# Gated feed-forward values brought to their partitions by 32x32 block transposes on VectorE and transfers within SBUF instead of TensorE transposes

## The reference, cut to what matters

```
def swiglu(h, w_in, w_out):
    gate, up = jnp.split(h @ w_in, 2, axis=-1)
    return (jax.nn.silu(gate) * up) @ w_out
```

## Time and profile before

| | us |
|---|---|
| Time, median of 3 executions | 1643.75 |
| Lowest and highest | 1642.6, 1644.36 |
| Profiled execution: its time | 1644.13 |
| Profiled execution: its span | 1642.0 |
| PE busy in the span | 1613.3 |
| DVE busy | 1039.4 |
| ACT busy | 817.1 |
| POOL busy | 570.8 |

### The profile page before, as it was taken

The page is one execution under the profiler, slowest core; times in us unless marked ns, Lnnn a source line. Parts: engine busy times, 40 slices in busy tenths (PEclk is TensorE's granted clock), DMA queues, the critical chain, the costliest instruction groups (busy, mean ns, idle before and its releaser), DMA issues.

```text
span 1642.0 us, 20828 instructions
## 1 busy us (share of the span) xinstructions
PE 1613.3 (98%) x7757; PEld 1334.1 (81%) x7757; DVE 1039.4 (63%) x1054; ACT 817.1 (50%) x983; POOL 570.8 (35%) x368
## 2 busy tenths in 40 slices
PE   6999999999999999999999999999999999999998
PEld 5888888978888788887878888888887888878887
DVE  5455568776665765567777765576667567774454
ACT  5455563354444534456655443553446666563433
POOL 0000100068991499920008897069990000000000
PEclk9999999999999999999999999999999999999999
DMA  7565653347776587864436787657784454545562
GB/s 258 182 201 179 230 175 113 123 146 251 245 250 209 175 260 245 259 213 154 145 112 204 259 258 247 202 186 254 238 269 153 154 166 150 172 152 184 185 196 77
DMA packets 208572, 321.48 MB, mean 196 GB/s; under 512 B 10952, under 2 KB 146434, under 8 KB 208514
## 3 DMA queue, kind: packets, MB, share of 16 engines
q1 hardware_dynamic: 196256, 281.05, 51.7%
q0 software_dynamic: 10512, 38.54, 7.5%
q10 hardware_dynamic: 1746, 1.11, 0.2%
HBM read 319.62 MB, written 1.05 MB: 195 GB/s over the span
## 4 chain that ended last, share of the span: by engine, by line
PE 92%; DVE 4%; ACT 2%; issue 1%; DMA 0%; ACTq 0%; SPq 0%; DVEq 0%
PE ps L557 27%; PE ps L559 26%; PE ps L558 26%; PE ps L603 3%; PE ps L848 2%; PE ps L661 2%; PE ps L611 2%; DVE w_lo L1820 1%; PE ps L565 1%; ACT w_hi L1299 1%; PE ps L1115 0%; ACT arena L1567 0%; DVE arena L1854 0%; DMA raw<-ffn_w_in_dram 0%; PE ps L980 0%
## 5 line engine op out<-in xcount | busy, mean ns | idle before, releaser
L1820 DVE TENSOR_TENSOR w_lo<-raw,w_hi 128x2048 fp32r<-128x2048 f32 x266 | 656.9, 2481 | 274.0 <-ACT w_hi L1299 273.8
L1299 ACT CAST w_hi<-raw 128x2048 fp32r<-128x2048 f32 x266 | 505.3, 1912 | 189.6 <-PE ps L559 187.4
L557 PE MATMUL ps<-w_hi,actT_hi 128*128 128x512 f32 x1456 | 578.2, 397 | 5.6 <-DVE hidden L1960 2.7
L559 PE MATMUL ps<-w_hi,actT_lo 128*128 128x512 f32 x1456 | 568.8, 391 | 0.0
L558 PE MATMUL ps<-w_lo,actT_hi 128*128 128x512 f32 x1456 | 567.8, 390 | 0.0
L557 PEld LDWEIGHTS ps<-w_hi,actT_hi 128*128 128x128 f32 x1456 | 274.0, 188 | 63.4 <-issue 5.7
L559 PEld LDWEIGHTS ps<-w_hi,actT_lo 128*128 128x128 f32 x1456 | 273.7, 188 | 58.6
L558 PEld LDWEIGHTS ps<-w_lo,actT_hi 128*128 128x128 f32 x1456 | 274.0, 188 | 54.0
L526 POOL TENSOR_TENSOR arena<-arena,c_silu 128x1024 f32<-128x1024 f32 x72 | 163.9, 2277 | 124.5 <-DVE actT_lo L1848 59.9
L557 PE MATMUL ps<-w_hi,hT_hi 128*128 128x512 f32 x480 | 187.5, 391 | 0.0
L559 PE MATMUL ps<-w_hi,hT_lo 128*128 128x512 f32 x480 | 186.8, 389 | 0.0
(11 more groups left out here) (258 smaller groups left out, 1323.3 us busy)
## 6 DMA issues: line engine op xcount, KB each, us to landing
raw<-ffn_w_in_dram SPq DMA_DIRECT2D x176, 512.0 KB, 4.8
raw<-ffn_w_out_dram SPq DMA_DIRECT2D x88, 512.0 KB, 4.4
arena<-w_ada_dram POOLq DMA_DIRECT2D x72, 512.0 KB, 5.5
raw<-ffn_w_gate_dram SPq DMA_DIRECT2D x44, 512.0 KB, 3.9
raw<-ffn_w_up_dram SPq DMA_DIRECT2D x44, 512.0 KB, 4.9
raw<-ffn_w_down_dram SPq DMA_DIRECT2D x44, 512.0 KB, 4.3
raw<-w_in_dram SPq DMA_DIRECT2D x40, 512.0 KB, 4.7
raw<-hg_w_in_dram SPq DMA_DIRECT2D x32, 512.0 KB, 4.7
```

The source lines that it names most:

```text
L557: nc.tensor.matmul(to, hi, whi, start=start, stop=False, skip_group_check=True)
L559: return nc.tensor.matmul(to, lo, whi, start=False, stop=stop, skip_group_check=True)
L1299: nc.scalar.copy(w_hi[:, s, :], raw[:, s, :]).then_inc(hi_ready[s], 1)
L1820: nc.vector.tensor_tensor(w_lo[:, s, :], raw[:, s, :], w_hi[:, s, :].bitcast(F32), ALU.subtract)\
```

## The change

The four TensorE transposes of each chunk but the last are gone. In their place:

- `product` writes the gated values in another order of the free dimension: it reads both operands with a stride of four elements and writes runs of 32, so that hidden columns with the same remainder modulo 4 stand together.
- `blocks` on DVE, right behind `product`, transposes the whole tile `hidden` in 32x32 blocks into a region of SBUF, `hid_blocks`.
- `to_columns` on ACT, at the end of the chunk, waits for it and issues four transfers of 64 KB each, SBUF to SBUF, each from 32 partitions to all 128, in pieces of 512 bytes, into `hT_raw`.
- `turned_hi` and `turned_lo` read `hT_raw` in SBUF instead of the PSUM bank. `turned_hi` waits for the transfers.

The last chunk of each sublayer still goes through TensorE. Some semaphores are merged or dropped at the start of the program without a new wait.

```diff
+        hid_blocks, hT_raw = (region(9600 + 512 * i, 4, P) for i in range(2))
+
+        def by_block(r):
+            return r.rearrange("p (f i b) -> p b f i", f=2, b=4)
+
+        def hidden_block(t):
+            return hidden.rearrange("p t f -> p (t f)").rearrange("p (b f t i) -> p t b f i", b=4, f=2, t=TILES)[:, t]
+
+        hT_columns = hT_raw.rearrange("p a (n j) -> p n a j", n=4)
...
-            pool.wait_ge(hT_turned, NF + 1)
+            pool.wait_ge(hT_turned, 2)
...
-                def turn_hidden(c):
-                    pe.wait_ge(hidden_ready, 2 * (n + c + 1))
-                    for f in range(2):
-                        for t in range(TILES):
-                            last = nc.tensor.transpose(ps[:, HT_BANK, f * T + t * P:f * T + (t + 1) * P],
-                                                       hidden[:, t, f * P:(f + 1) * P], ident)
-                    last.then_inc(hT_turned, 1)
...
                 def middle(c):
                     up(c, 0)
-                    turn_hidden(c - 1)
                     up(c, 1)
                     down(c - 1, False)
...
+                def to_columns(c):
+                    g = st.ffn * (NF - 1) + c
+                    act.wait_ge(hid_turned, g + 1)
+                    if positive(g):
+                        act.wait_ge(hT_ready, g)
+                    for a in range(4):
+                        nc.scalar.dma_start(hT_raw[:, a, :], hid_blocks[32 * a:32 * a + 32, :, :]).then_inc(hT_loaded, 16)
+
                 def turned_hi(c):
-                    act.wait_ge(hT_turned, st.ffn * (NF + 1) + c + 1)
-                    nc.scalar.copy(hT_hi[:, :, :], ps[:, HT_BANK, :].rearrange("p (f t) -> p f t", f=2)).then_inc(hT_hi_ready, 1)
+                    act.wait_ge(hT_loaded, 64 * (st.ffn * (NF - 1) + c + 1))
+                    if positive(filled[2] + c):
+                        act.wait_ge(split_used[2], filled[2] + c)
+                    nc.scalar.copy(hT_hi.rearrange("p f t -> p (f t)").rearrange("p (n a j) -> p n a j", n=4, a=4), hT_columns)\
+                        .then_inc(hT_hi_ready, 1)
...
                     split_hi(1, filled[1] + c + 1)
+                    to_columns(c)
...
+                def blocks(c):
+                    g = st.ffn * (NF - 1) + c
+                    dve.wait_ge(hidden_ready, 2 * (n + c) + 2)
+                    if positive(g):
+                        dve.wait_ge(hT_loaded, 64 * g)
+                    nc.vector.transpose(hid_blocks.rearrange("p b n -> p (b n)"), hidden.rearrange("p t f -> p (t f)"))\
+                        .then_inc(hid_turned, 1)
+
                 def turned_lo(c):
                     dve.wait_ge(hT_hi_ready, st.ffn * (NF - 1) + c + 1)
-                    nc.vector.tensor_tensor(hT_lo[:, :, :], ps[:, HT_BANK, :].rearrange("p (f t) -> p f t", f=2),
-                                            hT_hi[:, :, :].bitcast(F32), ALU.subtract).then_inc(hT_ready, 1)
-
-                def product(c):
+                    nc.vector.tensor_tensor(hT_lo.rearrange("p f t -> p (f t)").rearrange("p (n a j) -> p n a j", n=4, a=4), hT_columns,
+                                            hT_hi.bitcast(F32).rearrange("p f t -> p (f t)").rearrange("p (n a j) -> p n a j", n=4, a=4),
+                                            ALU.subtract).then_inc(hT_ready, 1)
+
+                def product(c, turn=True):
                     for t in range(TILES):
                         dve.wait_ge(gate_ready, 2 * (n + c) + t + 1)
-                        nc.vector.tensor_tensor(hidden[:, t, :], gate[:, t, :], ps[:, UP_BANK + t, FC:COLS], ALU.mult)\
-                            .then_inc(hidden_ready, 1)
+                        to, g, u = hidden[:, t, :], gate[:, t, :], ps[:, UP_BANK + t, FC:COLS]
+                        if turn:
+                            to, g, u = hidden_block(t), by_block(g), by_block(u)
+                        nc.vector.tensor_tensor(to, g, u, ALU.mult).then_inc(hidden_ready, 1)
+                    if turn:
+                        blocks(c)
```

More of the change, by code:

```diff
@@ L308, in build @@
         x_loaded = [sem("x_loaded0"), sem("x_loaded1")]
-        ident_loaded, rows_loaded, consts_loaded = sem("ident_loaded"), sem("rows_loaded"), sem("consts_loaded")
-        norms_loaded, levels_loaded = sem("norms_loaded"), sem("levels_loaded")
+        head_loaded, rows_loaded, consts_loaded = sem("head_loaded"), sem("rows_loaded"), sem("consts_loaded")
+        levels_loaded = sem("levels_loaded")
         small_loaded = sem("small_loaded")
@@ L316, in build @@
         zf_loaded, zf_rounded, zf_split = sem("zf_loaded"), sem("zf_rounded"), sem("zf_split")
-        lb_diff, levels_ready = sem("lb_diff"), sem("levels_ready")
+        levels_ready = sem("levels_ready")
         x_ready = sem("x_ready")
@@ L325, in build @@
         hT_turned, hT_hi_ready, hT_ready = sem("hT_turned"), sem("hT_hi_ready"), sem("hT_ready")
+        hid_turned, hT_loaded = sem("hid_turned"), sem("hT_loaded")
         hT_last_rounded, hT_last_ready = sem("hT_last_rounded"), sem("hT_last_ready")
@@ L337, in build @@
         post_half, post_sum = sem("post_half"), sem("post_sum")
-        post_sq, post_std, sqrt_loaded = sem("post_sq"), sem("post_std"), sem("sqrt_loaded")
+        post_sq, post_std = sem("post_sq"), sem("post_std")
         hg_turned, hg_q, hg_sig, hg_k = sem("hg_turned"), sem("hg_q"), sem("hg_sig"), sem("hg_k")
@@ L692, in ffn @@
                 after_second_chunk(st)
-                turn_hidden(0)
                 up(1, 1)
@@ L711, in ffn @@
                 up(NF - 1, 0)
-                turn_hidden(NF - 2)
                 up(NF - 1, 1)
@@ L1262, in token_mixer @@
                 branch_unit(1, 1, 1, lambda: turn_tile(by_name["tm_out"], tm_p[:, :, 3072:4096], 0))
-            pe.wait_ge(ident_loaded, 16)
-            pe.wait_ge(norms_loaded, 16)
+            pe.wait_ge(head_loaded, 32)
             nc.tensor.transpose(ps[:, SMALL_BANK, 0:48], rows_a[0:48, :], ident[0:48, 0:48]).then_inc(cols_turned, 1)
@@ L1356, in load_sqrt @@
             def load_sqrt():
-                nc.scalar.activation(sqrt_col, eps_col, ACT.Sqrt).then_inc(sqrt_loaded, 1)
+                nc.scalar.activation(sqrt_col, eps_col, ACT.Sqrt)
             def second_chunk(st):
@@ L1417, in ffn @@
                 split_hi(1, filled[1] + 1)
+                to_columns(0)
                 def middle(c):
@@ L1440, in last_hi @@
                 def last_hi(t):
-                    act.wait_ge(hT_turned, st.ffn * (NF + 1) + NF + t)
+                    act.wait_ge(hT_turned, 2 * st.ffn + t + 1)
                     if t:
@@ L1761, in vectors @@
                 nc.scalar.activation(c_silu[:, :], c_cols, ACT.Silu).then_inc(c_ready, 1)
-                act.wait_ge(lb_diff, 1)
+                act.wait_ge(cols_ready, 2)
                 nc.scalar.activation(lb[:, 1, :], lb[:, 0, :], ACT.Exp).then_inc(lb_exp, 1)
@@ L1768, in vectors @@
                 nc.scalar.copy(zf_hi[:, :, :], zf_raw[:, :, :]).then_inc(zf_rounded, 1)
-            nc.scalar.dma_start(ident, a["consts"][:, 0:P]).then_inc(ident_loaded, 16)
-            nc.scalar.dma_start(rows_a[0:48, :], a["norm_g"].rearrange("l i (k p) -> (l i k) p", p=P)).then_inc(norms_loaded, 16)
+            nc.scalar.dma_start(ident, a["consts"][:, 0:P]).then_inc(head_loaded, 16)
+            nc.scalar.dma_start(rows_a[0:48, :], a["norm_g"].rearrange("l i (k p) -> (l i k) p", p=P)).then_inc(head_loaded, 16)
             act.wait_ge(eps_ready, 1)
@@ L2003, in ffn @@
                 split_lo(3, filled[3] + 1)
-                product(NF - 1)
+                product(NF - 1, False)
                 last_lo(st, 0)
@@ L2486, in vectors @@
                 nc.vector.tensor_copy(lb[:, 2, :], lb_cols).then_inc(cols_ready, 1)
-                nc.vector.tensor_tensor(lb[:, 0, :], lb_cols, lb_cols, ALU.subtract).then_inc(lb_diff, 1)
+                nc.vector.tensor_tensor(lb[:, 0, :], lb_cols, lb_cols, ALU.subtract).then_inc(cols_ready, 1)
                 dve.wait_ge(lb_exp, 1)
```

## The result

| | us |
|---|---|
| Time after, median of 5 executions | 1626.39 (1624.65 to 1632.75) |
| Time before, taken beside it | 1643.74 (1642.6 to 1644.36) |
| Ratio, with its 95% interval | 0.9907 [0.9889, 0.9924] |
| Profiled execution after: time, span | 1630.87, 1629.1 |

The kernel became 17.4 us faster, with 1619.0 forecast. 28.5 us of transposes left TensorE, so 11.2 us were given back. The executions after lie 8 us apart, those before 1.8. The profiled one is 4.5 us above the median, so what its rows show as lost is more than the median lost.

What follows compares the result with a forecast made beforehand. TensorE was taken as the bound, 92% of the chain. 28.5 us removed less 1.3 at sublayer starts and 2.4 for GpSimd gives 24.8, so a median of 1619.0 us; 8-in-10 range 1615 to 1631.

Steps and rivals of the forecast that it cites:

- rival B: GpSimd becomes the bound in the third and fifth sublayers: up to 17.6 us lost, 1634; half gives 1626; chance 0.17.
- What is removed, 28.5 us: TensorE loses 60 transpose calls of 0.475 us each, slow restart included.
- The new way costs nothing in a steady chunk: Block transpose, four issues, landing, rounding and subtraction end near 101.2, before `down` at 108.5, so they cost nothing.
- The cover of 7.3 us before `down`: In a steady chunk the new path ends 7.3 us before `down`; a landing up to 11.6 us stays hidden.
- rival D: Transfers queue behind weight loads and each chunk waits, from landings of 12.1 us on: 1670 to 1700; chance 0.06.
- The strided product: nothing: Strided reads of `product` on DVE: even if doubled, 2 x 0.42 us more, DVE keeps idle time; nothing taken.
- The starts, 1.3 us lost: At sublayer starts PE waits more: 0.475 us in the third, 0.475 in the fifth, 0.35 for the others together.
- GpSimd, 2.4 us lost: At the fifth sublayer's end GpSimd finishes at 1238.3, the fold must begin by 1235.9, so PE waits 2.4 us.
- x: Time GpSimd loses in a sublayer to the new lock and closer spacing: 5 us taken, between 0 and 14.
- the allowances: Latest starts of the last fold without a PE wait: 1235.9 in the fifth sublayer, 714.2 in the third.
- the new lock: `hT_lo`, now with two SBUF inputs, shuts out GpSimd 0.69 us per chunk; 0.5 us per chunk taken as lost.
- closer spacing: Shorter chunks, 16.33 instead of 16.80 us, bring DVE's old locks on GpSimd closer together; part of GpSimd's lost time.

Runs made afterwards that it cites:

- the narrowed kernels: Kernels after and before, each with GpSimd's multiply and first two adds cut to 8 of 128 columns: 1612.34 us after, 1640.29 us before.
- the ceiling, e4: Kernel before without its 60 transpose calls and with nothing in their place, hidden values wrong: 1616.05 us.
- e7: Kernel after with each of the four transfers issued twice, the second copy into a spare region, and the wait covering all eight: 1709.83 us.
- e10: Kernel after with every transfer issued twice and GpSimd's arithmetic cut to 8 of 128 columns: 1688.68 us.
- e6: Kernel after with product's operands and result contiguous again, so hidden columns arrive in another order: 1628.15 us.
- e5: Kernel after with `hT_lo` reading a PSUM bank again instead of `hT_raw`, low parts wrong: 1624.18 us.
- e1: Kernel after with the sixth fold of sublayers two to five moved from behind chunk 9 to the sublayer's end: 1620.91 us.
- e8: Kernel after with only the last folds of the third and fifth sublayers moved, behind the sublayer's last product: 1620.29 us.

## Why the prediction came out as it did

The direction, the mechanism and the range were right; the point was 7.4 us too low, and the case that came is the forecast's own with rival B in part. Step by step:

- **What is removed, 28.5 us.** Confirmed: 27.95 between the narrowed kernels, 27.7 by the ceiling, -4.3 for 9 calls in the first and the sixth sublayer.
- **The new way costs nothing in a steady chunk.** Right in its result, wrong in its cover. The block transpose took 0.71 us (0.76 worked out), the landing 3.7 (4.3 taken), the four issues 2.52 (1.6 taken: a transfer of 128 pieces takes 0.63 us to issue, not 0.41). The cover of 7.3 us before `down` is real only for `down`. What binds first is the ring, which must close within 16.33 us. By the prediction's cover 1.6 + 11.6 = 13.2 us from the first issue to the end of the landing would be hidden; in e7 it was 11.1 us (656.12 to 667.18), and the time rose to 1709.8. With the 6.6 us that the ring of e10 needs behind the landing (7.2 in e7, with the locks), 16.33 - 6.6 = 9.7 us can be hidden, an estimate that the sixth sublayer of e7 bears out (median 9.0, at most 9.6). The kernel after needs a median of 6.1 to 6.6 us in the second to fifth sublayers and 8.6 at most. So it has 0.5 to 1 us to spare at its worst, not 7.3, and the point of rival D was too far out by some 3.5 us.
- **The strided product: nothing.** Right for the time: 0.2 us each, all in idle time of VectorE (e6).
- **The starts, 1.3 us lost.** About right: in the second and third sublayers together even e4 keeps 0.3 us less than 9.0, as does the second pair. The wait for `w_lo` at the third's start grew from 1.26 to 1.69. A few waits for `hT_lo` of 0.4 to 0.7 us came on top.
- **GpSimd, 2.4 us lost: the step that failed.** Five things in it. x was 6.2 us in the fifth sublayer and 8.2 in the third, where I took 5. The path behind the fold was 4.15 us in the sum and 6.8 on the chip (1226.51 to 1233.28), because the tile turn needs the last product, behind one more `w_lo`; this alone makes the allowances 2.6 us tighter in both sublayers, and is the largest error. The third sublayer, for which I had 2.4 us to spare, thus stalled for -2.4 + 3.2 + 2.6 = 3.4 us. In the fifth, on the other hand, the tile turn was due only 2.9 us earlier after GpSimd's start than before (161.2 us instead of 164.15), where I took 4.2; TensorE waited for `hT_lo` twice on the way (0.70 and 0.60 us). So 2.4 + 1.2 + 2.6 - 1.2 = 5.0. And the slow matmuls behind each wait, 1.6 and 2.3 us, were not in the sum. Together: waits 3.4 + 5.0 and slow matmuls 4.0 make 12.4 us in the profiled execution, where I had 2.4. The median lost less; its waits are not on record.
- **The reason for x.** The forecast put it on the new lock and on closer spacing. The lock is shown for the third sublayer (e5: 20.4 us of busy time, and -8.2 in the second and third sublayers instead of -3.5); the spacing is refuted (e4). In the fifth the lock is 2.0 of the 9.2 us between e4 and after, and the rest is not traced to a part of the change.

The Trainium skill (SBUF — State Buffer, Who interferes with whom) has the rule of two SBUF inputs on VectorE against GpSimd, and experiment 5 agrees: with one input in PSUM instead of SBUF the maximum of `hT_lo` falls from 2389 ns to 693. (The edit also drops the order of its columns, but that costs no time by itself: the least duration is 683 ns with it and 676 without.) By that rule `product`, with one input in PSUM, should not lock GpSimd, and the trace agrees: the 17 instructions of GpSimd that met it without another lock were not held up.

What stays open: why e1 and e8 still lack 4 to 5 us to e4. Waits of 0.4 to 1.4 us at boundaries are seen, but I did not try them one by one. And what makes GpSimd late in the fifth sublayer beside the lock of `hT_lo` is open too.

## What to carry to other kernels

When work leaves the bounding engine, ask which engines were already at its pace: a chunk 0.475 us shorter and a lock of 0.7 us were enough to let GpSimd, for which the last fold had waited 1.17 us at no cost, set the end of two sublayers. Follow the queue behind a wait to the instruction that the bounding engine really needs, not to the nearest one of the changed path; here that alone was 2.6 us. For a transfer in a loop, compare the whole ring (issues, landing, and what its wait holds up on the engine) with the period, not only the landing with its consumer; and place a wait for a slow helper where nothing stands behind it: moving two lines gave 6 us.

## What the hardware showed that I had not expected

- A wait of TensorE can cost more than its length: behind waits of 3.24 and 4.84 us the granted clock fell to its lower level, 1.2 GHz (matmuls 0.43 us apart instead of 0.23), for six and nine matmuls, and cost 1.6 and 2.3 us more. In e5, behind 3.56 us, seven matmuls were 0.43 us apart. Behind the 0.35 us wait of e8 it did not fall.
- An SBUF to SBUF transfer of 64 KB in 128 pieces took 0.63 us of ACT's queue to issue and landed after a median of 3.7 us: 2.5 and 2.2 in the first and sixth sublayers, 4.1 to 4.5 in the others, where `w_ada` is loaded too. Over all it was 2.6 in the run with GpSimd narrowed and 4.5 with twice as many.
- A product of 128x256 with strided operands took 610 ns instead of 414, and held no instruction of GpSimd up; nor did the block transpose of 711 ns, with its one input.
